# A two-block transformer kernel on one core: the first feed-forward opens with 8 plain weight tiles for 12, its residual goes through PSUM, and the first pairs are reordered

## The reference

```python
x = x + rms_norm(mixed @ w_out, norm_mix_post)
h = rms_norm(x, norm_ffn_pre)
f = (silu(h @ w_ffn_gate) * (h @ w_ffn_up)) @ w_ffn_down     # 1024 -> 2816 -> 1024
x = x + rms_norm(f, norm_ffn_post)
...
x = x + mix @ w_out_2
h = rms_norm_2(x, norm2_g_2)
x = x + (silu(h @ w_gate_2) * (h @ w_up_2)) @ w_down_2
```

## Time and profile before

| | us |
|---|---|
| median of 3 runs | 1427.36 |
| lowest and highest | 1425.91, 1427.73 |
| the profiled execution | 1427.21 |
| its span on the core | 1425.4 |
| TensorE busy | 1411.6 (99%) |
| VectorE, ScalarE, GpSimd busy | 814.3, 716.2, 797.8 |
| mean granted TensorE clock | 0.999 |

### The profile page before, as it was taken

One profiled execution on the slowest core, in us unless ns is written; L12 is line 12 of the kernel. 1 busy time (PEld: TensorE's weight loads), 2 busy tenths in 40 slices (PEclk: granted clock), 3 DMA queues, 4 the chain that ended last, 5 costly groups with the idle time before them and its releaser, 6 DMA issues.

```text
span 1425.4 us, 22206 instructions
## 1 busy us (share of the span) xinstructions
PE 1411.6 (99%) x8248; PEld 1206.0 (85%) x8248; DVE 814.3 (57%) x1426; ACT 716.2 (50%) x1254; POOL 797.8 (56%) x462
## 2 busy tenths in 40 slices
PE   9999999999999999999999999999999999999999
PEld 7888888888788877999998887877677899999887
DVE  5426656876535287677762436889765576764000
ACT  5243434766743255566652225766656566664221
POOL 4434423762254548777754546766237877775443
PEclk9999999999999999999999999999999999999999
DMA  6533221211133243323234334322124433323433
GB/s 193 150 90 87 88 62 45 60 59 48 58 89 104 89 133 119 102 91 119 92 116 134 104 105 138 112 74 66 42 76 146 132 104 105 114 95 121 130 104 118
DMA packets 40338, 143.03 MB, mean 100 GB/s; under 512 B 4688, under 2 KB 4944, under 8 KB 39728
## 3 DMA queue, kind: packets, MB, share of 16 engines
q1 hardware_dynamic: 38976, 139.08, 31.6%
q10 hardware_dynamic: 1264, 2.62, 0.6%
HBM read 135.40 MB, written 6.29 MB: 99 GB/s over the span
## 4 chain that ended last, share of the span: by engine, by line
PE 90%; DVE 6%; issue 1%; POOL 1%; ACT 1%; DMA 0%; SPq 0%; DVEq 0%; ACTq 0%
PE bank L1612 11%; PE bank L1614 11%; PE bank L1613 11%; PE bank L1965 8%; PE bank L1967 8%; PE bank L1966 8%; PE bank L1641 3%; PE bank L1643 3%; PE bank L1642 3%; PE bank L2072 3%; PE bank L2074 2%; PE bank L2073 2%; PE bank L1859 1%; PE bank L1894 1%; PE bank L1879 1%
## 5 line engine op out<-in xcount | busy, mean ns | idle before, releaser
L679 POOL TENSOR_TENSOR wL<-raw,wH 128x1024 fp32r<-128x1024 f32 x165 | 406.9, 2466 | 498.1 <-ACT wH L866 366.7
L866 ACT ACTIVATE wH<-raw 128x1024 fp32r<-128x1024 f32 x136 | 143.7, 1057 | 306.5 <-PE bank L1614 244.4
L1612 PE MATMUL bank<-aH,wH 128*128 128x512 f32 x376 | 148.9, 396 | 1.0 <-POOL wL L679 1.0
L1613 PE MATMUL bank<-aL,wH 128*128 128x512 f32 x376 | 146.7, 390 | 0.0
L1614 PE MATMUL bank<-aH,wL 128*128 128x512 f32 x376 | 146.6, 390 | 0.0
L1612 PE MATMUL bank<-fH,wH 128*128 128x512 f32 x352 | 137.1, 390 | 0.0
L1613 PE MATMUL bank<-fL,wH 128*128 128x512 f32 x352 | 137.0, 389 | 0.0
L1614 PE MATMUL bank<-fH,wL 128*128 128x512 f32 x352 | 137.0, 389 | 0.0
L1965 PE MATMUL bank<-aH,wH 128*128 128x256 f32 x408 | 115.4, 283 | 0.7 <-ACT ssum L1285 0.7
L1967 PE MATMUL bank<-aH,wL 128*128 128x256 f32 x408 | 115.3, 283 | 0.0
L1966 PE MATMUL bank<-aL,wH 128*128 128x256 f32 x408 | 115.2, 282 | 0.0
(11 more groups left out here) (456 smaller groups left out, 3852.5 us busy)
## 6 DMA issues: line engine op xcount, KB each, us to landing
raw<-in_w SPq DMA_DIRECT2D x200, 512.0 KB, 3.6
raw_too<-in_w SPq DMA_DIRECT2D x34, 512.0 KB, 3.8
kept_x<-xT SPq DMA_DIRECT2D x4, 1024.0 KB, 6.3
xT<-kept_x SPq DMA_DIRECT2D x8, 512.0 KB, 4.9
bmk<-in_bias SPq DMA_DIRECT2D x6, 512.0 KB, 4.8
out_x<-xT SPq DMA_DIRECT2D x8, 256.0 KB, 4.3
xT<-in_x SPq DMA_DIRECT2D x3, 512.0 KB, 8.2
ct<-in_ct ACTq DMA_DIRECT2D x3, 384.0 KB, 3.9
```

Source lines behind the costliest of these rows:

```text
L679: pool.tensor_tensor(wL[:, c_slot, :], raw[:, c_slot, :], wH[:, c_slot, :].bitcast(F32), ALU.subtract).then_inc(sem("w_lo"), 1)
L866: act.activation(wH[:, s, :], raw[:, s, :], ACT.Copy).then_inc(sem("w_hi"), 1)
L1612: pe.matmul(bank[:], hi, H[:, ka, :], start=(k == 0), stop=False)
L1613: pe.matmul(bank[:], hi, L[:, ka, :], start=False, stop=False)
```

## The change

gu1's opening has 8 tiles and so two more pairs. Around this:

- The residual of the first block: VectorE's multiply goes to a PSUM bank, its add reads it from there. VectorE no longer makes the low parts of the next input; GpSimd makes them from y. The squares are made by ScalarE within the loop, into PSUM bank 4, and VectorE sums them within the loop. TensorE takes the total before tile 4, not within it. Two of TensorE's idle products go to bank 4, so that the square can wait for them by a semaphore.
- GpSimd's order in gu1's opening is new.
- In gu2's opening ScalarE's order is new: y is made partly within the last projection, the root before the second chunk, and the sum is taken after one tile for two.
- In both first pairs, the order of TensorE's products and of ScalarE's copies is new.

```diff
-OPENING = {"gu1": 12, "gu2": 8}
+OPENING = {"gu1": 8, "gu2": 8}
...
             p = PH["gu1"]
-            opening_chunk(p, 2)
-            opening_chunk(p, 3)
+            for kt in range(KD):
+                pool.wait_ge(sem("h2_hi"), kt + 1)
+                pool.wait_ge(sem("pair_act"), after("y_made", kt + 1))
+                pool.tensor_tensor(aL[:, kt, :], y_work[:, kt, :], aH[:, kt, :].bitcast(F32), ALU.subtract).then_inc(sem("h2_lo"), 1)
+                if kt in (3, 5):
+                    opening_chunk(p, 2 + (kt - 3) // 2)
+            opening_chunk(p, 4)
             t_sum(p, 1)
...
-            for kt in range(KD):
-                square(2 * KD + kt, lambda: xT[:, kt, :])
-                if kt == 1:
-                    ahead(PH["gu1"], 2)
+                if kt == 0:
+                    act.wait_ge(sem("zeros_done"), 2)
+                act.wait_ge(sem("sq_used"), 2 * KD + kt)
+                act.activation(B[4][:], xT[:, kt, :], ACT.Square).then_inc(sem("sq_ready"), 1)
+            ahead(PH["gu1"], 2)
...
                 high_x22(base, 0)
-                high_f(p, first - 1)
+                t_high(p, 4, 4)
                 keep_p1(base, 0)
                 high_x11(base, 1)
-                t_high(p, 4, 4)
+                high_f(p, first - 1)
+                copy_x21(base, 1)
                 keep_u2(base, 0)
-                copy_x21(base, 1)
+                high_s4(base, 0)
                 high_s2(base, 1)
-                high_s4(base, 0)
...
-                    if mid is not None and t == 2:
+                    if mid is not None and t == (1 if p.name == "gu2" else 2):
                         mid()
...
                 p5(0)
-                p2(0)
                 pe.wait_ge(sem("pair_pool"), after("t_lo", 3 * stage_of(p) + 3))
                 p6(0)
+                p1(1)
                 p7(0)
-                for j in range(1, n):
+                p2(0)
+                pe.wait_ge(sem("pair_dve"), after("t4_lo", stage_of(p) + 1))
+                p4(0)
+                p6(1)
+                p3(0)
+                p2(1)
+                p7(1)
+                for j in range(2, n):
                     p1(j)
-                    if j > 1:
-                        p5(j - 1)
-                    else:
-                        pe.wait_ge(sem("pair_dve"), after("t4_lo", stage_of(p) + 1))
+                    p5(j - 1)
...
-            rest_of_opening(p, lambda k: total(3 * KD, B[5]) if k == 6 else None)
+            total(3 * KD, B[5])
+            rest_of_opening(p)
...
-            residual_and_low(zT, "g_mix_post", "res1", "h2", "g_ffn_pre", 1)
             clear_sum(2)
+            def sum_of_squares(n):
+                dve.wait_ge(sem("sq_ready"), n + 1)
+                dve.wait_ge(sem("sq_used"), n)
+                dve.tensor_tensor(ssum[:], B[4][:], ssum[:], ALU.add).then_inc(sem("sq_used"), 1)
+            dve.wait_ge(sem("root_spread"), 1)
             for kt in range(KD):
-                add_square(2 * KD + kt)
+                bank = B[6 + kt % 2]
+                dve.scalar_tensor_tensor(bank[:], zT[:, kt, :], vec("g_mix_post", kt), B[5][:], ALU.mult, ALU.mult)\
+                    .then_inc(sem("res1_mul"), 1)
+                dve.wait_ge(sem("res1_mul"), kt + 1)
+                dve.tensor_tensor(xT[:, kt, :], bank[:], xT[:, kt, :], ALU.add).then_inc(sem("res1"), 1)
+                if kt:
+                    sum_of_squares(2 * KD + kt - 1)
+            sum_of_squares(2 * KD + KD - 1)
```

## The result

The changed kernel takes 1430.62 us, the median of 9 runs (1428.45 to 1430.95). On the same chip the kernel before took 1427.36 (9 runs, 1424.90 to 1429.23). The ratio is 1.0024, 95% interval 1.0015 to 1.0033: slower by 0.24%. I had forecast 1424.4 and a range of 1420.8 to 1428.6, so the result lies above the range.

A forecast was written before the change was run, and what follows sets the result against it. TensorE, busy 1411.6 of 1425.4 us, was taken as the bound. Gains of 0.6 (first feed-forward), 1.2 (second opening) and 1.1 (second first pairs) made 2.9 us, so 1424.4 us, range 1420.8 to 1428.6.

The forecast's parts named there:

- Two features as pairs, and what they cost: gu1: four tiles become two pairs, gaining 1.6 us of TensorE work; with other gains and new waits, 0.6 net.
- the other estimate: gu1's opening: by the skill page's factor two, eight GpSimd lows take 11.8 us, not 10; up to 1.8 later, 1426.2.
- The sum of squares: gu1's opening: taking it within the residual loop removes a 2.5 us wait and 1.5 of slower clock, gain 4.0.
- PSUM operands: gu1's residual loop: VectorE's operations with one PSUM operand neither wait for GpSimd nor delay it; cost taken as 0.
- rival C: Residual loop: VectorE collides with GpSimd, 6.3 us later, 1430.7; also an ungaining second opening with two clock falls; chance 0.12.
- Second opening: gu2's opening: earlier root and sum, chunk 5's high part from 1097, no wait on it; gain 1.2 us.
- First pairs of gu2: Second feed-forward's first pairs: copies meet their products, only about 0.2 us of wait is new; gain 1.1 us.
- The sum again: Whole kernel: the forecast's total of gains, 0.6 + 1.2 + 1.1 = 2.9 us, making 1424.3 for the profiled execution.
- Rival A: TensorE's clock falls at the new waits, 1.5 us each: 1425.9 with one, 1427.4 with two; chance 0.23.

The follow-up runs named there:

- e4: The kernel before with only the new residual, 12 tiles kept, GpSimd's order putting each chunk's low part ahead of one sum: 1423.57 us, ratio 0.9978.
- e2: The changed kernel with the second opening's old ScalarE order and its sum asked for after two tiles: 1428.33 us, ratio 1.0006.
- e5: The changed kernel with one more wait: GpSimd's first sum of the second opening starts after VectorE's last sum of squares; 1427.05 us, ratio 0.9996.
- e6: The changed kernel with the old order of the first pairs: 1430.26 us, ratio 1.0025.
- e7: e4 plus the new order of the first pair in gu1 only: 1422.55 us, ratio 0.9970.
- e0: The kernel before, unchanged, once more: 1427.34 us, ratio 1.0004.
- e1: The kernel before with only the second opening's new ScalarE order, its sum taken one tile earlier: 1429.79 us, ratio 1.0017.
- e3: The kernel before with only the new order of products and copies in both first pairs: 1426.86 us, ratio 1.0003.
- e8: The changed kernel with seven eighths of the low parts of chunks 4 to 7 in gu1's opening left out: 1426.84 us, ratio 0.9998.
- e10: e8 with ScalarE's high parts of t1 to t3, its copy of x21 and VectorE's sums s1, s2 moved up: 1425.17 us, ratio 0.9990.
- e12: e7 plus the new second opening, GpSimd's first sum held behind VectorE's last sum of squares: 1421.40 us, ratio 0.9963.
- e13: e12 with chunk 5's high part ahead of feature 1's in the second opening: 1422.47 us, ratio 0.9966.

## Why the prediction was wrong

- *Two features as pairs, and what they cost.* The sum said 0.6 us net for gu1, the profiles show -0.1. The first product came 49.5 us after gu1's first matmul, where I had 48.7; behind it the rest took 184.6 us against 162.2, 22.4 more, exactly the 20.1 and 2.3 of the sum. The waits were met one by one: chunk 6 2.31 (2.1 forecast), x11 1.22 (1.4), p6 2.07 (2.4). GpSimd ran from the fifth chunk on as reckoned. This step was right in mechanism, and 0.7 off. Of that, 0.5 is there when GpSimd comes to the fifth chunk (525.69, 19.4 us behind gu1's first matmul; the sum had 18.9), after chunk 3's high part, which waits for TensorE to free its slot, had come 0.4 late. The rest lies between the end of x11's low part and the first product. The eight low parts took 1.30 us each, 1.26 start to start, 10 in all, as in the sum, and not the 11.8 of the other estimate.
- *The sum of squares.* The gain of 4.0 was nearly right: e4 shows 4.6 in gu1. But 1.5 of it was the clock, and I booked it as if a fall belonged to its wait. In the changed kernel's profile another came, in `in2`.
- *PSUM operands.* Right: VectorE's operations in the loop take 0.68 to 0.76, GpSimd's 1.30 and 2.40. The rival C got the sign and the time (1430.7) by a mechanism that did not occur. Its side remark, a second opening that doesn't gain, was the truth.
- *Second opening.* This is the step that failed. I had "Gain 1.2 us", the profiles show 1.24 lost. I called y's four tiles hidden in ScalarE's idle time, which they were, and didn't ask what an earlier y releases: GpSimd's sum, into VectorE's last sum of squares. The price stood in the earlier trace rows (2.12 beside GpSimd) and the earlier trace rows. I also took the first two features to be over when chunk 5's turn comes. Feature 1 needs tile 3; ScalarE was idle 4.04 us for it, chunk 5's high part came at 1102.99 and not at 1097 (1098.9 in this trace, whose opening starts 1.9 us later), and TensorE still waited 0.17 us for the low part:

```profile
1102.46 0.63 ACT L1214 ACTIVATE fH<-tmp 128x512 fp32r<-128x512 f32 x1 [4.04 <-DVE tmp L2789]
1102.99 1.05 ACT L867 ACTIVATE wH<-raw 128x1024 fp32r<-128x1024 f32 x1
1104.12 2.40 POOL L680 TENSOR_TENSOR wL<-raw,wH 128x1024 fp32r<-128x1024 f32 x1 [2.41 <-ACT wH L867]
```

- *First pairs of gu2.* "Gain 1.1 us" was 0.1. One reading was wrong: the 0.35 us that I put to the copy of p1 in the earlier trace rows belong to the line L1285, which is the copy of u3 ahead of p4 (p1's is L1277), and the new order doesn't take that wait away. Start to start, the 0.72 us for u2's copy went; the 0.5 for u3's grew to 0.77, and 0.3 for x11's low part came. The copy of u3 stands behind the high part of s2, which waited 2.35 us for VectorE. (The last row names a low part by GpSimd, which ended about then, but p4 waits in the program for the copy, which ended at 1132.69, and for a low part made long before.)

```profile
1131.82 0.60 ACT L1223 ACTIVATE wH<-bank 128x512 fp32r<-128x512 f32 x1 [2.35 <-DVE bank L2807]
1132.31 0.38 ACT L1287 ACTIVATE ssum<-bank 128x256 f32<-128x256 f32 x1
...
1132.83 0.35 PE L1961 MATMUL bank<-aH,wH 128*128 128x256 f32 x1 [0.61 <-POOL wL L762]
```

- *The sum again.* 0.7 in gu1, 2.4 in the second opening, 1.0 in gu2's pairs and 1.6 for the clock make 5.7 of the 6.2 us between 1424.3 and the profiled execution's 1430.47.
- *Rival A* put falls at the new waits. Of the four profiles with the 2.3 us wait for chunk 6 (the changed kernel, e2, e5, e6) two have one behind it, e2 (and a second behind its wait of 2.03 us before p6) and e5. So waits shorter than the old 2.5 us can be followed by one. But gu1 is only 0.5 and 0.04 us longer there, not 1.5 a fall: TensorE was ahead of GpSimd, and what it lost it no longer waited at the first product, where neither e2 nor e5 shows a wait.

## What to carry to other kernels

Before taking work from the engine that bounds the kernel, add up what the helper beside it must still do in the shorter time; here TensorE's time fell by 21.7 us where GpSimd had 6 us of slack and some 10 less to do, and in place of a gain of 1.6 us gu1 grew by 5.5. When an operation is moved earlier, follow what it releases on the next engine, and look whether that runs into a VectorE operation with two SBUF inputs (here 0.68 us became 2.85). Try the parts of a change one by one: the residual and the new pairs' order in gu1 were worth 0.3% (e7), and the 8 tiles and the second opening ate it.

## What the hardware showed that I had not expected

Falls of the clock to 1.2 GHz aren't bound to one place. The 2.5 us wait for the sum in gu1 was followed by one in all four profiles that had it (before, e0, e1, e3), the 2.3 us wait for chunk 6 in two of four, the wait of about 2 us before p6 in one of four (e2; not in the changed kernel, e5 and e8), the 1.8 us wait of the second opening in three of five (e6, e8, e10; not in e1 and the changed kernel). Five came without a long wait, near 860 us (e2, e4) and 980 us (changed kernel, e1, e7). What TensorE did before the one at 983 us in the changed kernel:

```profile
979.70 1.95 PE L2084 MATMUL bank<-ct,sq 128*128 128x2 f32 x16 [0.26 <-ACT sq L1399]
981.51 0.48 PE L2073 MATMUL bank<-aH,wH 128*128 128x512 f32 x1
```

Sixteen matmuls of 2 columns, 1.8 us in which it counts as busy. Shortly before those near 860 us stand 16 matmuls of 1 and 2 columns. The same rows stand in every profile, mostly without a fall behind them; e12 and e13, which have neither long wait, show none anywhere. The page "TensorE: Matmul & The Clock Gate" of the Trainium skill, section "What's actually happening", ties the lower level to an idle engine. In the changed kernel TensorE is busy for 12.54 of the 12.8 us before the fall (970 to 982.8) and for 8.00 of 8.00 us in the row of 980 to 988, so busy time in a profile doesn't say whether the clock holds. What decides between one execution and the next stays open.

The two instructions that collide don't pay alike: GpSimd's went from 2.38 to 2.82 us, VectorE's from 0.68 to 2.85.
